# A transformer kernel on one core: twelve matmuls of an output projection placed inside the retention loop

## The reference

```python
ret = bidirectional_retention(to_bhsd(rq), to_bhsd(rk), to_bhsd(rv), ...)
ret = rms_norm(ret, ret_norm_w[l].reshape(RET_HEADS, HEAD_DIM)).reshape(B, S, RET_WIDTH)
y_ret = jax.nn.silu(rg) * ret
h = h + jnp.concatenate([y_attn, y_ret], axis=-1) @ w_out[l]
```

## Time and profile before

| what | us |
|---|---|
| median of 3 runs | 2755.48 |
| lowest and highest run | 2753.03 and 2758.49 |
| span of the profiled execution | 2756.5 |
| TensorE (PE) busy in it | 2702.0 |
| VectorE (DVE) busy | 1719.8 |
| POOL busy | 1518.5 |
| ScalarE (ACT) busy | 1059.7 |

### The profile page before, as it was taken

How to read it: one execution, slowest core, us unless ns; L and a number is a source line. 1 busy time by engine, 2 the same in 40 slices (tenths; PEclk the granted TensorE clock), 3 DMA queues, 4 the chain that set the end, 5 groups by cost and what they waited for, 6 DMA issues and landing times.

```text
span 2756.5 us, 37485 instructions
## 1 busy us (share of the span) xinstructions
PE 2702.0 (98%) x13788; PEld 2191.8 (80%) x13788; DVE 1719.8 (62%) x2578; ACT 1059.7 (38%) x2084; POOL 1518.5 (55%) x1148
## 2 busy tenths in 40 slices
PE   7999999999999999999999999999999999999998
PEld 6777788878888888777777788888788788888886
DVE  6776755687777777723355741143368777767777
ACT  5644422343444444423343511021254444444444
POOL 3232243477887878532222244455614788787884
PEclk9999999999999999999999999999999999999999
DMA  3001102111111211130101011131101212121112
GB/s 136 31 31 37 38 17 92 54 54 58 58 62 58 69 54 58 51 117 31 39 32 40 32 46 54 53 122 62 69 24 46 65 53 63 58 70 54 58 54 80
DMA packets 102774, 157.18 MB, mean 57 GB/s; under 512 B 6992, under 2 KB 60752, under 8 KB 101456
## 3 DMA queue, kind: packets, MB, share of 16 engines
q1 hardware_dynamic: 97472, 133.19, 14.5%
q10 hardware_dynamic: 5136, 21.76, 2.1%
HBM read 146.54 MB, written 8.39 MB: 56 GB/s over the span
## 4 chain that ended last, share of the span: by engine, by line
PE 91%; DVE 3%; POOL 2%; issue 1%; ACT 1%; DMA 1%; ACTq 0%; SPq 0%; DVEq 0%; POOLq 0%
PE PS L1346 13%; PE PS L1347 13%; PE PS L1348 13%; PE PS L1000 12%; PE PS L1002 11%; PE PS L1001 11%; PE PS L1120 1%; PE PS L1038 1%; PE PS L1041 1%; PE PS L1039 1%; PE PS L1109 1%; PE PS L1488 1%; PE PS L1380 1%; PE PS L1135 1%; PE PS L1374 1%
## 5 line engine op out<-in xcount | busy, mean ns | idle before, releaser
L821 POOL TENSOR_TENSOR WH<-WRAW,CST 128x512 fp32r<-128x512 f32 x204 | 226.5, 1110 | 838.9 <-PE PS L1002 725.7
L1000 PE MATMUL PS<-XH,WH 128*128 128x512 f32 x1248 | 513.4, 411 | 2.9 <-POOL WL L823 2.0
L1002 PE MATMUL PS<-XH,WL 128*128 128x512 f32 x1248 | 490.0, 393 | 0.0
L1001 PE MATMUL PS<-XL,WH 128*128 128x512 f32 x1248 | 488.8, 392 | 0.0
L3035 DVE TENSOR_TENSOR H<-H,PS 128x512 f32<-128x512 f32 x560 | 367.3, 683 | 41.9 <-PE PS L1348 41.7
L856 POOL TENSOR_TENSOR WL<-WRAW,WH 128x512 fp32r<-128x512 f32 x174 | 251.4, 1446 | 118.2 <-ACT WH L2058 88.8
L1000 PEld LDWEIGHTS PS<-XH,WH 128*128 128x128 f32 x1248 | 235.3, 189 | 82.8 <-issue 36.8
L823 POOL TENSOR_TENSOR WL<-WRAW,WH 128x512 fp32r<-128x512 f32 x204 | 271.3, 1330 | 16.0
L1002 PEld LDWEIGHTS PS<-XH,WL 128*128 128x128 f32 x1248 | 235.0, 188 | 51.4
L1001 PEld LDWEIGHTS PS<-XL,WH 128*128 128x128 f32 x1248 | 235.9, 189 | 41.9 <-issue 0.5
L856 POOL TENSOR_TENSOR WL<-XX,WH 128x512 fp32r<-128x512 f32 x148 | 202.0, 1367 | 92.9 <-ACT WH L2058 92.5
(11 more groups left out here) (371 smaller groups left out, 5416.0 us busy)
## 6 DMA issues: line engine op xcount, KB each, us to landing
WRAW<-ws SPq DMA_DIRECT2D x104, 512.0 KB, 3.5
WRAW<-ws SPq DMA_DIRECT2D x120, 256.0 KB, 2.6
XX<-ws SPq DMA_DIRECT2D x108, 256.0 KB, 2.7
RAWX<-ws SPq DMA_DIRECT2D x56, 256.0 KB, 2.6
H<-xT ACTq DMA_DIRECT2D x4, 1024.0 KB, 11.0
H<-xT ACTq DMA_DIRECT2D x2, 2048.0 KB, 11.1
h_spill<-H ACTq DMA_DIRECT2D x1, 4096.0 KB, 12.9
H<-h_spill ACTq DMA_DIRECT2D x4, 1024.0 KB, 8.5
```

The costliest lines, as they stand in the source:

```text
L821: pool.tensor_tensor(WH[:, j, c], WRAW[:, j, c], ONES[:, 0:1].to_broadcast((P, 512)), ALU.mult).then_inc(hi_split, 1)
L1000: pe.matmul(out, WH[:, j, w], rh(kt), start=(n == 0), stop=False)
L1001: pe.matmul(out, WH[:, j, w], rl(kt), start=False, stop=False)
L1002: last = pe.matmul(out, WL[:, j, w], rh(kt), start=False, stop=(n == len(kts) - 1))
```

## The change

Twelve matmuls, the three products of unit 22's k-tiles 0 to 3 in the first half of the tokens, leave `first_units` and stand in turn 5 of the retention loop (`early_product`). The high and low parts of k-tiles 0 to 3 are made one in each turn of the loop, on ScalarE ahead of the turn's copy and on VectorE behind the turn's fold: turns 0 to 3 make the first half of the tokens, turns 4 to 7 the second. The high and low parts of tiles 4 to 7 stay behind the loop, in the order of the halves, and the counts that TensorE waits for follow the new order (`y_place`). For this, qx and FST move from XH's place to XL's, tiles 4 to 7 (QL). The loads of H stand ahead of the remaining high parts.

```diff
+            QL = sb(st, "QL", [P, KT, S])
...
-        FST = QS[:, 0, half(1)].rearrange("p (a j d) -> p a j d", a=2, j=4)
+        FST = QL[:, 4, half(1)].rearrange("p (a j d) -> p a j d", a=2, j=4)
...
-            return QS[:, 2 * (c % 2) + d, half(0)].rearrange("p (j b) -> p j b", j=4)
+            return QL[:, 4 + 2 * (c % 2) + d, half(0)].rearrange("p (j b) -> p j b", j=4)
...
+        def y_place(kt, h):
+
+            return 8 * (kt // 4) + 4 * h + kt % 4
...
+                            if (xs, h, u) == (XS_Y1, 0, u0) and kt < 4:
+                                continue
...
+            def early_product(kt):
+
+                if kt == 0:
+                    pe.wait_ge(unit_split, 2 * U_WO1 + 1)
+                w = blk(kt)
+                pe.wait_ge(x_high, XS_Y1 + y_place(kt, 0) + 1)
+                pe.matmul(PS[:, 0], WH[:, 0, w], XH[:, kt, half(0)], start=(kt == 0), stop=False)
+                pe.matmul(PS[:, 0], WL[:, 0, w], XH[:, kt, half(0)], start=False, stop=False)
+                pe.wait_ge(x_split, XS_Y1 + y_place(kt, 0) + 1)
+                pe.matmul(PS[:, 0], WH[:, 0, w], XL[:, kt, half(0)], start=False, stop=False)
...
                     if c == 5:
+                        early_product(0)
                         r_sums(0, 2)
+                        early_product(1)
                     r_inner(c + 1)
                 if c == 5:
                     r_sums(0, 3)
+                    early_product(2)
                 r_outs(c)
+                if c == 5:
+                    early_product(3)
...
+            act.wait_ge(o_out, 32)
             for c in range(NB):
+                kt, h = c % 4, c // 4
+                if kt == 0:
+                    act.wait_ge(full[2 + h], uses[U_WO1 - 1][2 + h] + 1)
+                high(XH[:, kt, half(h)], Q1[:, kt, half(h)])
                 r_copy(c)
...
-            for n in range(16):
-                kt, h = n % 8, n // 8
+            act.dma_start(H[:, 0:4], xT[:, 0:4]).then_inc(x_in, 16)
+            act.dma_start(H[:, 4:8], xT[:, 4:8]).then_inc(x_in2, 16)
+            for n in range(8):
+                kt, h = 4 + n % 4, n // 4
                 if n == 4:
                     r_square(1)
-                    act.dma_start(H[:, 0:4], xT[:, 0:4]).then_inc(x_in, 16)
-                    act.dma_start(H[:, 4:8], xT[:, 4:8]).then_inc(x_in2, 16)
-                if n == 8:
                     r_roots(1)
-                if kt >= 4:
-                    act.wait_ge(r_norm, 4 * h + kt - 3)
-                high(XH[:, kt, half(h)], (Q1[:, kt] if kt < 4 else RQ[:, kt - 4])[:, half(h)])
+                act.wait_ge(r_norm, n + 1)
+                high(XH[:, kt, half(h)], RQ[:, kt - 4, half(h)])
...
+                low(XL[:, kt, half(h)], Q1[:, kt, half(h)], XH[:, kt, half(h)])
                 if c >= 6:
                     r_norms(c - 6)
```

More of the change, by code:

```diff
@@ L1036, in first_units @@
                                 pe.wait_ge(unit_split, 2 * u + 1 + kt // 4)
-                            pe.wait_ge(x_high, xs + 8 * h + kt + 1)
+                            n = y_place(kt, h) if xs == XS_Y1 else 8 * h + kt
+                            pe.wait_ge(x_high, xs + n + 1)
                             pe.matmul(PS[:, bank], WH[:, j, w], XH[:, kt, half(h)], start=(kt == 0), stop=False)
                             pe.matmul(PS[:, bank], WL[:, j, w], XH[:, kt, half(h)], start=False, stop=False)
-                            pe.wait_ge(x_split, xs + 8 * h + kt + 1)
+                            pe.wait_ge(x_split, xs + n + 1)
                             last = pe.matmul(PS[:, bank], WH[:, j, w], XL[:, kt, half(h)], start=False, stop=(kt == KT - 1))
@@ L2832, in _ @@
                     r_inverse(0)
+                kt, h = c % 4, c // 4
+                if c == 1:
+                    dve.wait_ge(full[2], uses[U_WO1 - 1][2] + 1)
+                if kt == 0 and h:
+                    dve.wait_ge(full[3], uses[U_WO1 - 1][3] + 1)
+                low(XL[:, kt, half(h)], Q1[:, kt, half(h)], XH[:, kt, half(h)])
                 if c >= 6:
@@ L2835, in _ @@
             r_norms(2)
-            for n in range(16):
-                kt, h = n % 8, n // 8
+            for n in range(8):
+                kt, h = 4 + n % 4, n // 4
                 if n == 2:
                     r_norms(3)
-                if n == 8:
+                if n == 4:
                     r_inverse(1)
-                if n >= 12:
-                    r_norms(n - 8)
-                low(XL[:, kt, half(h)], (Q1[:, kt] if kt < 4 else RQ[:, kt - 4])[:, half(h)], XH[:, kt, half(h)])
+                if n >= 4:
+                    r_norms(n)
+                low(XL[:, kt, half(h)], RQ[:, kt - 4, half(h)], XH[:, kt, half(h)])
             dve.wait_ge(r_sum, 2)
```

## The result

The changed kernel takes 2763.64 us, median of 15 runs (2757.36 to 2771.44), against 2756.22 us for the kernel before, also over 15 (2752.97 to 2760.86). The ratio is 1.0031 with a 95% interval of 1.0023 to 1.0038, so it is slower, by 7.4 us, which is 0.3% of the time. The profiled execution has a span of 2761.7 us, 5.2 above the one before.

A forecast was written before the change was run, and what follows sets the result against it. The prediction took TensorE, busy 98% of 2756.5 us, as the bound. Its terms, 0 + 2.5 - 3.4 + 3.4 = +2.5 us, gave a span of 2759.0, less 1.0 to the median: 2758.0 us, range 2752.5 to 2764.5.

The forecast's parts named there:

- rival B: Stall at the projection's head makes a long slow stretch, turn 5 gets nothing back: +7.6 us, 2763.1; chance 0.25.
- Moved products, parts one a turn, queues: Retention loop: twelve moved matmuls zero net, high and low parts covered by idle time, SP's and POOL's queues unaffected: 0 us.
- Head and wait, +2.5: Output projection's head: gaps of 0.60 us go, TensorE newly stalls 3.1 us for the late squares: +2.5 us.
- Clock in turn 5, -3.4: Retention loop, turn 5: a short half-clock stretch costing 1.7 us replaces the long one costing 5.1: -3.4 us.
- Clock at the head, +3.4: Output projection's head: the clock falls at the new wait and statistics groups, between 1.7 and 5.1 us: +3.4 us.

The follow-up runs named there:

- x4: The changed kernel with the four squares ahead of the high parts of tiles 4 to 7 and the twelve early products back at the head: 2756.96 us, ratio 1.0000.
- x1: The changed kernel with the four squares put ahead of the high parts of tiles 4 to 7 on ScalarE: 2757.16 us, in a second set 2754.90 us.
- x2: The changed kernel without the twelve early products, which stand at the head again, squares still late: 2761.70 us, ratio 1.0023.
- x6: The changed kernel, squares still late, with the four statistics groups two k-tiles later: 2760.74 us, ratio 1.0013.
- x3: The changed kernel with the squares first, as in x1, and the four statistics groups two k-tiles later: 2753.50 us, in a second set 2756.11 us.
- x5: The changed kernel with twelve unused matmuls of 512 columns filling the wait ahead of r_sums(1, 0): 2759.96 us, ratio 1.0005.

## Why the prediction was wrong

The time, 2763.64, lay in the range, but the forecast was a difference too small to measure (+2.5), and what came is nearest to rival B, +7.4 against its +7.6. B holds on average only: in the first profile of the change turn 5 did get its clock back, and the head was slow for longer than B said. The sign and the order of events were right. What failed are two terms of the sum, both of them clock: -3.4 for turn 5, where the profiles give -0.6, and +3.4 for the head, where they give +6.2. Each is off by 2.8 us, and both the same way.

- *Moved products, parts one a turn, queues:* right. In turns 1 to 4 the change adds no wait of TensorE; a turn still takes 5.2 us.
- *Head and wait, +2.5:* right. 2.88 of wait less 0.60 of gaps is +2.3 us, by the chain that was named (forecast: a wait of 3.1). The run with the squares first shows that their place is the cause.
- *Clock in turn 5, -3.4:* wrong. The step took the 10.24 us of one profile as what every execution loses. The three profiles of before have 10.2, 3.4 and 3.4 us, a mean cost of 2.8; those of the change 0, 13 and 0, a mean cost of 2.2. By the runs without the early products (x4 against x1, x2 against x6) the products bring 1 to 1.6 us in median, not 3.4, and even that is within the noise. The step also held that products which come too late to prevent the fall would probably end the stretch sooner; in the two profiles where they came too late it lasted 13 us.
- *Clock at the head, +3.4:* right in sign, half in size. The term was a value between 1.7 and 5.1 without a measured case of a wait with groups behind it. The three stretches of 17, 10 and 10 us cost 6.2 on average. The reason given, that more groups lie in what follows, fits the timeline, where triples and groups alternate at half clock from 417.74 to 429.84 and the full clock returns only at about 434, some 4 us after the end of the last group. (Between the third and fourth group stand six products, not the three that the prediction read.) That the thin triples matter by themselves, without a wait, is not shown (x1 against x3); the slow stretch in x5's profile, which began amid them with only 0.17 us of wait, speaks for it.
- The sum of the measured terms, +2.3 - 0.6 + 6.2 = +7.9, meets the 7.4 us of the medians. Two of the three are means of three profiles each that differ by 7 to 14 us of half clock, so part of this agreement is luck.

The rule quoted from the Trainium skill ("TensorE: Matmul & The Clock Gate", section "Why this matters for your kernels", idle gaps between bursts drop the clock) pointed the right way at the head: the three profiles of the change have 10 to 17 us at half clock behind a gap of 2.9 us, and the eight profiles without a wait for the square (three of before, x1, x3, x4) are at 1.00 there. The gaps that the section speaks of are slightly longer than this one. With a gap of 1.5 us one profile kept full clock (x6) and one did not (x2), and in x5 the gap was filled and the slow stretch came all the same.

The place that the prediction took for a gap that leaves the clock alone was a draw too. The gap of 2.7 us at 580.8 to 583.8 passed at full clock in all three profiles of before; in all three of the change the clock fell at the same gap. The row of the first:

```profile
587.50:591.00 3.50, 3.48 (x8) 0.51 0.24 75
```

That is 3.4 us at half clock, with nothing but triples behind the gap. Behind the gap of 2.9 us at the head, with the groups following it, it was 10 to 17. This speaks for the thin work as what makes the stretch long; no run isolates it.

What stays open: how the loss at the head divides between the length of the wait and the thinness of the work behind it. The wait of 1.5 us (x6) cost 3.8 us of mean time against none (x3), with a standard error of 1.4; the change cost 5.3 more than x6, with one of 1.7, and x6 has its groups further apart as well.

No version beats the kernel before beyond its interval. The best by median are the two with the squares first, 0.5 us under the 2755.9 of before.

## What to carry to other kernels

When steps move to an earlier place, look at what they leave behind: here the twelve products had also been the cover for a chain over three engines, and the statistics that had stood ahead of a waiting copy on ScalarE stood behind it afterwards. Price a new wait of TensorE with the clock that it may take along, which here was over twice the wait itself. And a slow stretch seen in one profile is one draw: look at several executions before counting it as a gain.

## What the runs showed of the hardware

- One and the same program had 10.2, 3.4 and 3.4 us at half clock in the same place in three executions; the changed one 0, 13 and 0. The place at which the clock falls is not fixed by the program.
- The clock stayed at half through 16 us in which TensorE had no idle time at all (417.74 to about 434 us of the changed kernel). In the first 12 of them groups of two-column products alternate with triples of 512 columns; the last 4 have triples alone.
- The clock fell inside a wait in one profile (by 417.00, the wait ended at 417.74) and amid the two-column groups, 3 us after a wait of 0.17 us, in another (x5, at about 422.3).
- Twelve useless matmuls in place of an equally long wait made the kernel some 5 us faster (means of 2758.9 and 2764.3).
